# A bias scratch without copies, read backwards, and another PSUM ring for the second attention's weighted values

## The reference

```python
bias_gr = rel_bias.T.reshape(G, R, REL_BUCKETS)
s_c = einsum(qb, kc) + bias_gr[:, :, t5_bucket(tq[:, None] - cend[None, :])]   # compressed keys
# selected keys, window keys: scores + bias_gr[..., t5_bucket(t - s)], causal mask, softmax, times values
```

## Time and profile before

| | us |
|---|---|
| median of three executions | 1624.25 |
| the three | 1624.05, 1629.16, 1624.25 |
| profiled execution, its own time | 1631.8 |
| its span, first to last instruction | 1630.0 |
| mean granted TensorE clock | 0.976 |

### The profile page before, as it was taken

How to read it: one execution, slowest core, us unless ns; L and a number is a source line. 1 busy time by engine, 2 the same in 40 slices (tenths; PEclk the granted TensorE clock), 3 DMA queues, 4 the chain that set the end, 5 groups by cost and what they waited for, 6 DMA issues and landing times.

```text
span 1630.0 us, 24997 instructions
## 1 busy us (share of the span) xinstructions
PE 1547.4 (95%) x10255; PEld 1389.8 (85%) x10255; DVE 1030.4 (63%) x1704; ACT 797.5 (49%) x1437; POOL 229.8 (14%) x189
## 2 busy tenths in 40 slices
PE   9999999898998999999989999999988799999999
PEld 6899889698986889988879998797876699989887
DVE  5765586675856575469578774645655486666643
ACT  4545445364643446535446653453445564455531
POOL 2300032211201130032021110012010041100000
PEclk9989999999999989999999999999989899999999
DMA  8633355359664534246345554655211244645453
GB/s 312 234 104 104 91 193 207 107 194 192 219 211 158 203 106 152 79 142 223 129 167 172 186 203 165 211 184 187 91 45 49 78 141 152 218 156 181 156 185 125
DMA packets 41025, 261.31 MB, mean 160 GB/s; under 512 B 4512, under 2 KB 5152, under 8 KB 14672
## 3 DMA queue, kind: packets, MB, share of 16 engines
q1 hardware_dynamic: 35600, 238.44, 42.7%
q0 software_dynamic: 2944, 15.69, 3.7%
q10 hardware_dynamic: 2368, 5.58, 0.9%
HBM read 254.98 MB, written 4.19 MB: 159 GB/s over the span
## 4 chain that ended last, share of the span: by engine, by line
PE 71%; DVE 13%; ACT 7%; issue 4%; DMA 3%; POOL 1%; ACTq 0%; POOLq 0%; DVEq 0%; SPq 0%
PE ps L484 62%; DVE lows L1547 5%; ACT wh L1027 3%; PE ps L594 3%; DMA raw<-d_wst 3%; PE ps L675 1%; DVE ar L2078 1%; ACT S L1450 1%; PE ps L696 1%; ACT arR L1528 1%; POOL sm L2276 1%; DVE xTr L1566 1%; DVE S L2259 1%; PE ps L714 1%; DVE S L2140 1%
## 5 line engine op out<-in xcount | busy, mean ns | idle before, releaser
L1547 DVE TENSOR_TENSOR lows<-raw,wh 128x1024 fp32r<-128x1024 f32 (+3 forms) x473 | 544.6, 1170 | 266.8 <-ACT wh L1027 264.2
L484 PE MATMUL ps<-xTr,wh 128*128 128x256 f32 (+2 forms) x3472 | 637.3, 286 | 10.5 <-DVE lows L1547 8.5
L484 PEld LDWEIGHTS ps<-xTr,wh 128*128 128x128 f32 (+2 forms) x3472 | 540.7, 191 | 16.2 <-issue 8.5
L1027 ACT CAST wh<-raw 128x1024 fp32r<-128x1024 f32 (+3 forms) x473 | 455.2, 989 | 193.7 <-DMA raw<-d_wst 163.6
L484 PE MATMUL ps<-xTr,lows 128*128 128x256 f32 (+1 forms) x1736 | 492.7, 284 | 0.0
L484 PEld LDWEIGHTS ps<-xTr,lows 128*128 128x128 f32 (+1 forms) x1736 | 331.5, 191 | 0.0
L484 PE MATMUL ps<-wh,arR 128*128 128x512 f32 x928 | 299.5, 401 | 7.5 <-DVE ar L1732 3.6
L484 PEld LDWEIGHTS ps<-wh,arR 128*128 128x128 f32 x928 | 176.5, 190 | 53.2 <-DVE ar L1732 5.4
L484 PE MATMUL ps<-lows,arR 128*128 128x512 f32 x464 | 185.2, 399 | 0.0
L484 PE MATMUL ps<-wh,xTr 128*128 128x512 f32 x480 | 155.4, 400 | 17.7 <-DVE xTr L1566 13.2
L484 PE MATMUL ps<-arR,wh 128*128 128x256 f32 (+1 forms) x832 | 149.3, 281 | 0.0
(11 more groups left out here) (259 smaller groups left out, 1538.8 us busy)
## 6 DMA issues: line engine op xcount, KB each, us to landing
raw<-d_wst SPq DMA_DIRECT2D x196, 1024.0 KB, 4.9
raw<-d_wst SPq DMA_DIRECT2D x24, 512.0 KB, 3.5
raw<-d_wst SPq DMA_DIRECT2D x12, 896.0 KB, 4.6
raw<-d_wst SPq DMA_DIRECT2D x8, 672.0 KB, 4.7
ar<-d_lnp POOLq DMA_DIRECT2D x5, 1024.0 KB, 5.0
raw<-d_wst SPq DMA_DIRECT2D x8, 441.0 KB, 3.5
d_scr<-PT POOLq DMA_DIRECT2D x1, 3072.0 KB, 36.2
ar<-d_par POOLq DMA_DIRECT2D x2, 1192.0 KB, 9.5
```

The source lines that it names most:

```text
L484: op = e.matmul(out, s, m, start=start and i == 0, stop=stop and i == len(pairs) - 1)
L1027: e.copy(high_of(m), raw_of(m)).then_inc(*high.done(m))
L1547: e.tensor_tensor(low_of(m), raw_of(m), high_of(m).bitcast(F32), ALU.subtract).then_inc(*low.done(m))
```

## The change

The one-hot table is built for rising distance, with 127 masked places ahead of distance 0 and masked places behind distance 255. The scratch holds one row of 384 for each head (24 KB). It is written once, without copies, and read with a partition step of 1, 16 rows of 256 for each partition (2 MB, as before). The table in `TB` then rises along the keys' axis, and the three reads of it go backwards, through `back`: a step of -1 in L2140, of -16 in L2104. The weighted values `pv2` take their bank from `M` instead of `A`, with the same event that frees it.

```diff
 def bias_tables():
     m = np.arange(512)
-    dist = 255 - m
-    ok = dist >= 0
+    dist = m - 127
+    ok = (dist >= 0) & (dist < T)
+def back(t, first, n, step=1):
+    a = T - 1 - first
+    z = a - step * (n - 1) - 1
+    return t[..., a:z if z >= 0 else None:-step]
@@ tensor, second attention, finish(un)
-                    b = A.take(w, ("pv2", i, un), vec, "o2", i, un)
+                    b = M.take(w, ("pv2", i, un), vec, "o2", i, un)
@@ vector
-                bc = TB[:, :, first:first + 16 * (ncv - 1) + 1:16]
+                bc = back(TB, first, ncv, 16)
-  e.tensor_tensor_reduce(Sv[:, hold + h, 0:nk], bv[:, k, 0:nk], TB[:, 4 * hq + h, soff:soff + nk], 1.0,
+  e.tensor_tensor_reduce(Sv[:, hold + h, 0:nk], bv[:, k, 0:nk], back(TB[:, 4 * hq + h, :], soff, nk), 1.0,
-                                    A["pv2", i, un][:, 0:256].rearrange("p (h d) -> p h d", d=64),
+                                    M["pv2", i, un][:, 0:256].rearrange("p (h d) -> p h d", d=64),
@@ gpsimd
-  e.dma_start(scr_d, PT[0:16, 1024:1408].unsqueeze(1).to_broadcast([16, 128, 384]))
+  e.dma_start(scr_d, PT[0:16, 1024:1408])
-  e.dma_start(TB, bass.AP(scr_d.tensor, 127, [[383, 128], [128 * 384, 16], [1, 256]]))
+  e.dma_start(TB, bass.AP(scr_d.tensor, 0, [[1, 128], [384, 16], [1, 256]]))
@@ kernel
-    scr = dram("scr", [16, 128, 384], "Internal")
+    scr = dram("scr", [16, 384], "Internal")
```

More of the change, by code:

```diff
@@ L2354, in gpsimd @@
                         w.wait_ge(vec, "rel")
-                        e.dma_start(scr_d, PT[0:16, 1024:1408].unsqueeze(1).to_broadcast([16, 128, 384])).then_inc(*bias_out.done())
+                        e.dma_start(scr_d, PT[0:16, 1024:1408]).then_inc(*bias_out.done())
                 if l == 0:
@@ L2387, in gpsimd @@
             first_block_done()
-            e.dma_start(TB, bass.AP(scr_d.tensor, 127, [[383, 128], [128 * 384, 16], [1, 256]])).then_inc(*bias_in.done())
+            e.dma_start(TB, bass.AP(scr_d.tensor, 0, [[1, 128], [384, 16], [1, 256]])).then_inc(*bias_in.done())
             for i in range(2):
```

## The result

The changed kernel takes 1611.42 us in the median of four executions (1609.05 to 1612.2), against 1624.15 of four of the kernel before: a ratio of 0.9916, 95% interval 0.9889 to 0.9942. Measured once more later, beside other kernels, the ratio was 0.991 (0.9894 to 0.9926), with a median of 1609.53 against 1625.59. The forecast of 1610.1 (1604 to 1620), faster, held.

The account below looks back on a forecast made before the run. The prediction took TensorE, busy for 95% of the span, as the bound. Its terms, 9.4 us for the write and 4.7 us for the ring, summed to 14.1 us: 1610.1 us against the median of 1624.25, range 1604 to 1620.

Parts of the forecast that it names:

- The write, 9.4 us: Layer 0's feed-forward part: writing 24 KB instead of 3 MB removes TensorE's gap and the slow stretch, minus 9.4 us.
- the gap: Near 400 us, beside the 3 MB write: TensorE stands still for 6.92 us as the weight-group ring runs dry.
- The rival that the gap is small outside the profile: At the write: gap smaller in ordinary executions, leaving 1.9 + 4.7 = 6.6 us, 1617.6; chance 15%.
- The table's read and the step of -1, nothing: Reading the 2 MB table back and L2140's reversed operand on VectorE: neither changes the time.
- The rival in which the gap moves to the read: Reversed table's read at 1031 holds up the stream as the write did: 4.7 us left, 1619.6; chance 6%.
- The bound from L2104's row, 7.1 us: VectorE's L2140: reversed step costs at most 7.1 us; as a rival, 7.0 us gain left, 1617.2, chance 10%.
- The rule on 16-byte lines: L2140's reversed read: accesses within one 16-byte line run at full bandwidth, so the step of -1 costs nothing.
- The ring, 4.7 us: Second attention, i = 1: pv2 from ring M ends the wait loop with o2; VectorE's waits go, minus 4.7 us.
- The rival that VectorE's wait stays: Second attention: TensorE late with the transposes, so the ring moves little: 9.4 us gain, 1614.8; chance 10%.
- VectorE with ScalarE's exponentials as the next bound: Second attention, i = 1: this loop sets 7.1 us a unit; TensorE waits some 0.7 us for exponentials.
- i = 0, nothing, and no new wait in ring M: Second attention: no gain in i = 0, where VectorE is the bound; ring M's added waits cost nothing.
- The sum: Whole kernel: 9.4 + 4.7 = 14.1 us saved, 1610.1 against the median of 1624.25.

Follow-up runs that it names:

- copies back: The changed kernel with each head's row again written 128 times (3 MB), only the first copy read: 1621.46 us, ratio 0.9969 to the kernel before.
- scratch alone: The changed kernel with its ring part undone, pv2 taking its bank from ring A as before: 1616.67 us, ratio 0.9938 to the kernel before.
- ring alone: The kernel before with only pv2's bank moved to ring M, 3 MB write and forward reads kept: 1620.74 us, ratio 0.9966.
- second tile alone: The changed kernel with pv2 of query tile i = 0 back in ring A, only i = 1 from ring M: 1611.37 us, ratio 0.9901.
- busy shift: The changed kernel with 11 plain products of 512 columns added ahead of step n = 8 of layer 0's feed-forward part: 1620.68 us, ratio 0.9968.

## Why the prediction was right

- **The write, 9.4 us: right.** Aligned by TensorE's instructions, the kernel before falls 9.4 us behind the changed one across the gap: the products before the gap lie 1.4 us apart in the two profiles, those at 408 us 10.8. Removing only the part gave a ratio of 0.9938, 10.1 us; adding back only the 3 MB write 0.9969 against the changed kernel's 0.9916 or 0.991, 8.6 or 9.6 us. The rival that the gap is small outside the profile (1.9 us left) falls. What filled the 7.5 us between the profiled execution and the median can thus not have been this gap. The slow stretches of the last section don't explain it either: the profiled execution of copies back has them too, and its 1620.0 us lie below that kernel's median.
- **The table's read and the step of -1, nothing: right.** 9.6 us of landing, 281 and 425 ns. The rival in which the gap moves to the read falls too: between 860 and 1130 us the two profiles stay 13.0 to 13.1 us apart. The bound from L2104's row, 7.1 us, was far off, and its working was loose, as L2104 reads PSUM and L2110, from which I took the time without the step, does not. The rule on 16-byte lines gave zero (the Trainium skill, SBUF — State Buffer, "Door 1: The DMA port swizzle"), and the trace agrees as far as this one step goes.
- **The ring, 4.7 us: right, a little low.** From the first copy of i = 1 to the last weighted values, the distance between the two profiles grows by 5.3 us, and by 6.0 against the scratch alone; the ring alone gave 5.5 by its ratio, and 5.3 between its profile and that of the kernel before. The term was the idle time of the copies alone. An instruction that follows without a wait also overlaps the one before by some 0.07 us (`o2` to copy, 0.34 us from start to start at 0.42 us duration), six times: 0.4 us, which makes 5.1; and the scratch alone had longer waits of its own (5.4 us against 4.7). The rival that VectorE's wait stays falls.
- **VectorE with ScalarE's exponentials as the next bound: right.** 7.0 us a unit for the forecast 7.1, TensorE idling 0.5 for 0.7. I had not named that TensorE also waits ahead of the weighted values in three more units (0.7, 1.5 and 1.5 us, beside the last unit's 3.6, where before only the last unit waited for the copy, 3.7). They lie on the same chain, as the copy they wait for comes late behind a cast's low part. That the last unit ends on this copy was in the prediction.
- **i = 0, nothing, and no new wait in ring M: right.** In no row does TensorE wait for ScalarE's L1419, which frees the steps' banks; the second tile alone is as fast.
- **The sum.** 14.1 us forecast; 12.7 in the first medians, 16.1 in the later ones. The range held both. That it lies between the two says little, as they are 3.4 us apart; the terms rest on the rows and on the parts run alone.

## What to carry to other kernels

Judge a transfer off the critical path by what it does to the stream beside it: here 3 MB in one write cost 9.4 us and the same 3 MB in eight parts nothing, because each weight group landed in 5.4 us beside the parts and in some 20 beside the one write, and a ring of four groups, each used for 5.8 us, covers a landing of some 17 us (the estimate above). When a ring of banks is shared, count takes per period: with five takes on four banks each take inherits another kind's release, and a late reader stalls a step that has nothing to do with it. After removing such a wait, look at what the other side's loop takes, waits for a third engine included; and work that is held back needs a place where nothing waits for it, as a cast behind it can cost more than the wait that was removed.

## What the runs showed that I had not expected

The profiled spans differ by 20.9 us where the two terms give 9.4 + 5.3. Of the rest, some 4 us lie at two later places. What is left are single short stretches at the lower clock that fall into one profile and not into the other; the 1.4 us ahead of the gap are one. Granted clock (the number ahead of the last two) between 505 and 540 us and between 575 and 610 us, first before:

```profile
505.00:540.00 35.00, 30.28 (x124) 23.56 (x123) 21.10 (x29) 10.06 (x16) 10.03 (x5) 0.90 0.46 154
575.00:610.00 35.00, 34.41 (x224) 30.06 (x223) 26.71 (x46) 15.29 (x29) 14.29 (x9) 0.85 0.27 91
```

then the changed kernel:

```profile
505.00:540.00 35.00, 30.26 (x138) 24.10 (x137) 21.81 (x26) 16.09 (x22) 9.38 (x5) 1.00 0.60 210
575.00:610.00 35.00, 34.23 (x238) 30.26 (x237) 24.58 (x55) 17.89 (x39) 5.21 (x4) 0.90 0.27 91
```

and busy shift, where TensorE is as late but has no gap:

```profile
505.00:540.00 35.00, 30.27 (x136) 23.88 (x135) 24.14 (x31) 12.53 (x18) 10.02 (x5) 1.00 0.49 180
575.00:610.00 35.00, 34.39 (x235) 30.67 (x234) 27.91 (x56) 16.51 (x36) 12.30 (x8) 0.90 0.36 121
```

The three profiles with the gap (before, ring alone, copies back) all have 0.90 and 0.85 there; all eleven without it have 1.00 and 0.90, busy shift among them. So a place some 130 us after TensorE stood still runs at 1.2 GHz for a time, and being late alone does not do it. That is some 4 us in the profile (2.8 and 1.1 to 1.5, between instructions aligned as above). What carries the gap's mark that far I can't say; no run looked for it.

The medians hardly show it: they give the gap 8.6 to 9.6 us, with an interval of some 3 us on either side, and not the profile's 13 to 14; that is as much as the delay of busy shift without any standing still. The mean granted clock is known for every execution: 0.9806 over the eight of copies back, 0.9840 over the eight of the changed kernel. As time at the lower clock (twice the difference, times 1620 us) that is 11 us more. The stretches above have 6.6 us of it behind the gap and 17 with both later places. So the later places may show in a part of the executions; this is an estimate, with an error of 2 to 3 us, and doesn't settle it.
